# HGRN2/RWKV-7 trunk on Trainium2: where PE issues the RWKV side products around the inverse's levels, and where DVE makes the HGRN2 states

## The reference, cut to what matters

```
def step(state, inp):
    rt, wt, kt, vt, kkt, at = inp
    sa = jnp.einsum('bhvk,bhk->bhv', state, -kkt)
    state = state * wt[:, :, None, :] + sa[..., None] * (kkt * at)[:, :, None, :] + vt[..., None] * kt[:, :, None, :]
    return state, jnp.einsum('bhvk,bhk->bhv', state, rt)
```

```
o = jnp.einsum('bhts,bhsv->bhtv', attn, vc) + jnp.einsum('bhtk,bhkv->bhtv', qc * jnp.exp(G), state)
state = jnp.exp(g_last[:, :, 0, :, None]) * state + jnp.einsum('bhsk,bhsv->bhkv', kc * jnp.exp(g_last - G), vc)
```

## Time and profile before

| | us |
|---|---|
| median of 3 runs (lowest, highest) | 1282.61 (1280.92, 1283.79) |
| the profiled execution's own time | 1283.81 |
| its span, from the first to the last instruction | 1281.7 |
| PE busy in it | 1160.3 (91%) |
| DVE, POOL, ACT busy | 756.7, 618.4, 440.1 |

### The profile page before, as it was taken

The page is one execution under the profiler, slowest core; times in us unless marked ns, Lnnn a source line. Parts: engine busy times, 40 slices in busy tenths (PEclk is TensorE's granted clock), DMA queues, the critical chain, the costliest instruction groups (busy, mean ns, idle before and its releaser), DMA issues.

```text
span 1281.7 us, 31323 instructions
## 1 busy us (share of the span) xinstructions
PE 1160.3 (91%) x12058; PEld 927.3 (72%) x12058; DVE 756.7 (59%) x1344; ACT 440.1 (34%) x827; POOL 618.4 (48%) x584
## 2 busy tenths in 40 slices
PE   2898999999999999999996889997899999989995
PEld 1777877778778777787784768876677777768873
DVE  7556575475565754756554331348656776867547
ACT  4342343242422423334324410123425243442223
POOL 3643442443425424434242147777456574738771
PEclk9999999999999999999998979999899999999997
DMA  5221121211112212111121033333122222212321
GB/s 200 75 68 43 54 65 29 73 53 42 54 41 67 62 28 66 51 42 60 35 68 48 27 115 110 96 91 90 54 78 83 68 88 65 82 57 83 92 89 65
DMA packets 46726, 88.39 MB, mean 69 GB/s; under 512 B 5808, under 2 KB 6832, under 8 KB 46384
## 3 DMA queue, kind: packets, MB, share of 16 engines
q1 hardware_dynamic: 44352, 82.37, 21.9%
q10 hardware_dynamic: 2288, 4.72, 1.1%
HBM read 84.97 MB, written 2.10 MB: 68 GB/s over the span
## 4 chain that ended last, share of the span: by engine, by line
PE 73%; DVE 16%; issue 5%; ACT 4%; DMA 1%; DVEq 0%; SPq 0%; ACTq 0%
PE psum L329 72%; ACT mix L950 4%; DVE mix L1366 3%; DVE mix L1390 2%; DVE mix L1461 1%; PE psum L887 1%; DVE mix L1892 1%; DVE mix L1810 1%; DVE h_split L1370 1%; DVE mix L1821 1%; DVE mix L1884 1%; DVE mix L1875 1%; DVE mix L1890 1%; DMA mix<-xT 1%; DVE y L1896 1%
## 5 line engine op out<-in xcount | busy, mean ns | idle before, releaser
L329 PE MATMUL psum<-h_split,w_hi 128*128 128x512 f32 x2320 | 750.8, 405 | 31.2 <-DVE mix L1468 12.8
L329 PEld LDWEIGHTS psum<-h_split,w_hi 128*128 128x128 f32 x2320 | 429.2, 191 | 141.4 <-issue 42.2
L312 POOL TENSOR_SCALAR w_hi<-w_raw 128x512 fp32r<-128x512 f32 x290 | 208.1, 718 | 613.2 <-PE psum L329 472.8
L329 PE MATMUL psum<-h_split,w_lo 128*128 128x512 f32 x1160 | 457.6, 394 | 0.0
L314 POOL TENSOR_TENSOR w_lo<-w_raw,w_hi 128x512 fp32r<-128x512 f32 x290 | 410.8, 1417 | 24.2
L329 PE MATMUL psum<-mix 64*64 64x64 f32 (+5 forms) x8256 | 282.1, 238 | 40.8 <-DVE mix L1461 15.0
L329 PEld LDWEIGHTS psum<-mix 64*64 64x64 f32 (+3 forms) x8256 | 241.2, 139 | 97.3 <-issue 69.4
L950 ACT ACTIVATE mix<-psum 128x512 f32<-128x512 f32 (+4 forms) x292 | 139.9, 495 | 432.6 <-PE psum L329 323.1
L329 PEld LDWEIGHTS psum<-h_split,w_lo 128*128 128x128 f32 x1160 | 220.5, 190 | 48.5
L950 ACT ACTIVATE mix<-mix 128x512 f32<-128x512 f32 (+2 forms) x266 | 137.8, 549 | 196.9 <-DVE mix L1793 73.5
L1461 DVE COPY_PREDICATED mix<-mask,psum 128x128 f32<-128x128 uint8 (+1 forms) x192 | 83.0, 469 | 70.1 <-PE psum L329 56.2
(11 more groups left out here) (115 smaller groups left out, 658.4 us busy)
## 6 DMA issues: line engine op xcount, KB each, us to landing
w_raw<-wall SPq DMA_DIRECT2D x290, 256.0 KB, 2.6
mix<-xT SPq DMA_DIRECT2D x4, 512.0 KB, 5.4
mix<-xT ACTq DMA_DIRECT2D x1, 2048.0 KB, 8.0
out<-mix SPq DMA_DIRECT2D x8, 256.0 KB, 2.1
mix<-mask_f SPq DMA_DIRECT2D x1, 1728.0 KB, 11.1
mix<-pT ACTq DMA_DIRECT2D x2, 512.0 KB, 4.0
mix<-lru_w ACTq DMA_DIRECT2D x4, 256.0 KB, 3.4
mix<-w2a ACTq DMA_DIRECT2D x16, 32.0 KB, 2.1
```

The lines of the kernel that those rows point to most:

```text
L312: pool.tensor_scalar(w_hi[:, slot, :, :], w_raw[:, slot, :], 1.0, 0.0, ALU.mult, ALU.add).then_inc(sem["w_hi"], 1)
L329: return pe.matmul(o, lhsT, rhs, start=start, stop=stop, skip_group_check=True)
```

## The change

PE's order around the inverse, with the loop written out; `products(r, k_t)` is cut into two halves (`key_products`), two `token_rows` and `value_rows` go between levels; the `pe.sem_inc(tile_groups, 1)` of eleven functions and the semaphore are gone (shown once):

```diff
-                    for n in range(4):
-                        token_rows(r, n, head)
+                    token_rows(r, 0, head)
+                    token_rows(r, 1, head)
                     inverse_pt(r, 1, 0)
                     inverse_pt(r, 1, 1)
-                    products(r, k_t)
-                    with pe.Fori(1, 5) as lvl:
+                    key_products(r, 0)
+                    inverse_n(r, 1, 0)
+                    inverse_n(r, 1, 1)
+                    key_products(r, 1)
+                    for lvl in range(2, 5):
+                        inverse_pt(r, lvl, 0)
+                        inverse_pt(r, lvl, 1)
+                        if lvl == 4:
+                            value_rows(r)
                         inverse_n(r, lvl, 0)
                         inverse_n(r, lvl, 1)
-                        inverse_pt(r, lvl + 1, 0)
-                        inverse_pt(r, lvl + 1, 1)
-                    value_rows(r)
-                    state_sums(r, True)
+                        if lvl < 4:
+                            token_rows(r, lvl, head)
+                    inverse_pt(r, 5, 0)
+                    inverse_pt(r, 5, 1)
                     inverse_last(r, 0)
                     inverse_last(r, 1)
+                    state_sums(r, True)
                     output_sums(r, True)
```

The token rows in the order v, b, k, a, in banks 1, 0, 1, 0 (so that `inverse_pt` of level 1 needs none of them), and the new functions:

```diff
-                elif n == 3 and head:
-                    pe.wait_ge(sem["free0"], freed(r + 1, 2))
                 elif n == 1:
-                    pe.wait_ge(sem["rw_ops"], count("rw_ops", r, 3))
-                    pe.wait_ge(sem["hg_n"], count("hg_n", r))
-                o = bank[(1, 4, 5, 0)[n]]
+                    if head:
+                        pe.wait_ge(sem["free0"], freed(r + 1, 2))
+                else:
+                    pe.wait_ge(sem["rw_tok"], count("rw_tok", r, n - 2))
+                    if n == 2:
+                        pe.wait_ge(sem["rw_ops"], count("rw_ops", r, 3))
+                o = bank[(1, 0, 1, 0)[n]]
...
+            def scores(r, keys, p):
+
+                for e in range(2):
+                    for g in range(2):
+                        last = mm(bank[2 + e][rows[g], p * P:(p + 1) * P], keys[rows[e], tokens(2 * p + g)], ar[rows[e], g, p, :, :])
+                return last
...
+            def key_products(r, half):
+
+                if half == 0:
                     pe.wait_ge(sem["rw_masked"], count("rw_masked", r, 2))
-                pe.sem_inc(tile_groups, 1)
...
+                    pe.wait_ge(sem["rw_ops"], count("rw_ops", r, 3))
+                for p in (2 * half, 2 * half + 1):
+                    last = scores(r, k_t, p)
+                if half:
+                    last.then_inc(sem["rw_qk"], 1)
```

DVE has `upto` ahead of its first `inverse_pt` copy, and the states ahead of v's lerp:

```diff
+                    upto(r)
                     inverse_pt(r, 1, 0)
-                    upto(r)
                     inverse_pt(r, 1, 1)
...
+                    states(i)
                     mixed(i, 2, 7, wv)
-                    states(i)
```

More of the change, by code:

```diff
@@ L135, in trunk @@
         stored = ctx.enter_context(nc.semaphore("stored"))
-        tile_groups = ctx.enter_context(nc.semaphore("tile_groups"))
         vector_copies = ctx.enter_context(nc.semaphore("vector_copies"))
@@ L445, in token_rows @@
                         last = mm(o[:, at], wv[:, at], centre)
-                    elif n == 2:
+                    elif n == 3:
                         g, grp = p // 2, p % 2
@@ L449, in token_rows, with products @@
                     else:
-                        last = pe.transpose(o[:, at], (k_t if n == 1 else b_t)[:, at], ident)
+                        last = pe.transpose(o[:, at], (b_t if n == 1 else k_t)[:, at], ident)
                 last.then_inc(sem["rw_tr"], 1)
[L453 to L459, removed]
-                    pe.wait_ge(sem["rw_masked"], count("rw_masked", r, 2))
-                pe.sem_inc(tile_groups, 1)
[L462 to L467, removed]
+            def scores(r, keys, p):
[3 more added lines that the diff above has]
+                return last
+            def products(r):
+                pe.wait_ge(sem["rw_ops"], count("rw_ops", r, 2))
+                if not is_first(r):
+                    pe.wait_ge(sem["rw_norm"], count("rw_norm", r - 1, 0))
+                for p in range(4):
+                    last = scores(r, b_t, p)
+                last.then_inc(sem["rw_qk"], 1)
+            def key_products(r, half):
+                if half == 0:
+                    pe.wait_ge(sem["rw_masked"], count("rw_masked", r, 2))
+                    pe.wait_ge(sem["rw_ops"], count("rw_ops", r, 3))
+                for p in (2 * half, 2 * half + 1):
+                    last = scores(r, k_t, p)
+                if half:
+                    last.then_inc(sem["rw_qk"], 1)
             def turned_products(r):
@@ L490, in inverse_pt @@
             def inverse_pt(r, lvl, grp):
-                if isinstance(lvl, int) and lvl == 1:
-                    if grp == 0:
-                        pe.wait_ge(sem["rw_tok"], count("rw_tok", r, 2))
+                if lvl == 1 and grp == 0:
+                    pe.wait_ge(sem["hg_n"], count("hg_n", r))
                 pe.wait_ge(sem["rw_x"], count("rw_x", r, 2 * (lvl - 1) + grp))
-                pe.sem_inc(tile_groups, 1)
                 for e, q, g, p in in_group(grp):
@@ L526, in value_rows @@
                 pe.wait_ge(sem["rw_masked"], count("rw_masked", r, 4))
-                pe.wait_ge(sem["rw_tok"], count("rw_tok", r, 3))
-                pe.sem_inc(tile_groups, 1)
+                pe.wait_ge(sem["rw_tok"], count("rw_tok", r, 0))
                 for grp in range(2):
                     for e, q, g, p in in_group(grp):
-                        last = mm(bank[g][rows[q], P * grp + 64 * e:P * grp + 64 * e + 64], rw_m[rows[g], e, p, 4, :],
+                        last = mm(bank[2 + g][rows[q], P * grp + 64 * e:P * grp + 64 * e + 64], rw_m[rows[g], e, p, 4, :],
                                   v_tok[rows[g], e, p, :])
@@ L535, in state_sums @@
             def state_sums(r, first):
-                pe.sem_inc(tile_groups, 1)
+                if first:
+                    pe.wait_ge(sem["rw_ge"], count("rw_ge", r))
+                    pe.wait_ge(sem["rw_tok"], count("rw_tok", r, 2))
                 for p in range(4):
@@ L691, in embedding @@
                         if m == 2:
-                            pe.wait_ge(sem["rw_ge"], count("rw_ge", r))
+                            pe.wait_ge(sem["rw_tok"], count("rw_tok", r, 3))
                         embed(0, m, U_PRJ0, (0, 1))
@@ L713, in even_round @@
                 if pair:
-                    products(r, b_t)
+                    products(r)
                     turned_products(r)
-                    for n in range(4):
-                        token_rows(r, n, head)
+                    token_rows(r, 0, head)
+                    token_rows(r, 1, head)
                     inverse_pt(r, 1, 0)
                     inverse_pt(r, 1, 1)
-                    products(r, k_t)
-                    with pe.Fori(1, 5) as lvl:
+                    key_products(r, 0)
[7 more added lines that the diff above has]
+                            value_rows(r)
                         inverse_n(r, lvl, 0)
                         inverse_n(r, lvl, 1)
-                        inverse_pt(r, lvl + 1, 0)
-                        inverse_pt(r, lvl + 1, 1)
-                    value_rows(r)
-                    state_sums(r, True)
+                        if lvl < 4:
+                            token_rows(r, lvl, head)
+                    inverse_pt(r, 5, 0)
+                    inverse_pt(r, 5, 1)
                     inverse_last(r, 0)
                     inverse_last(r, 1)
+                    state_sums(r, True)
                     output_sums(r, True)
@@ L1050, in token_rows @@
                 act.wait_ge(sem["rw_tr"], count("rw_tr", r, n))
-                if n == 2:
-                    f(ga.rearrange("p g r e s t -> p (g r e) s t")[:, :, 1, :], bank[5].rearrange("p (c t) -> p c t", t=64),
+                if n == 3:
+                    f(ga.rearrange("p g r e s t -> p (g r e) s t")[:, :, 1, :], bank[0].rearrange("p (c t) -> p c t", t=64),
                       ACT.Copy).then_inc(sem["rw_tok"], 1)
                     return
-                dst = (v_tok, rw_m[:, :, :, 3, :], None, rw_m[:, :, :, 2, :])[n]
-                f(dst, bank[(1, 4, 5, 0)[n]].rearrange("p (c e t) -> p e c t", e=2, c=4), ACT.Copy).then_inc(sem["rw_tok"], 1)
+                dst = (v_tok, rw_m[:, :, :, 2, :], rw_m[:, :, :, 3, :])[n]
+                f(dst, bank[(1, 0, 1)[n]].rearrange("p (c e t) -> p e c t", e=2, c=4), ACT.Copy).then_inc(sem["rw_tok"], 1)
             def inverse_pt(r, lvl, grp):
@@ L1066, in value_rows @@
                 f(ga.rearrange("p g r e s t -> p g (r e) s t")[:, :, :, 0, :],
-                  psum[:, 0:2, 0:256].rearrange("p g (n t) -> p g n t", t=64), ACT.Copy).then_inc(sem["rw_ge"], 1)
```

(8 more changed lines are left out.)

9 lines of the change are left out of this document (1 added, 8 removed).

## The result

| | us | ratio to before, 95% interval |
|---|---|---|
| before, median of 8 runs | 1282.57 | |
| changed, median of 8 runs (1270.95 to 1278.22) | 1276.23 | 0.9943 [0.9926, 0.9961] |
| predicted | 1256.5 (1240 to 1274) | |

What follows compares the result with a forecast made beforehand. It took PE's waits for copies and masks in the inverse's serial levels, and for DVE's states at round ends, as the bound. 1283.8 - 23 (parts 1 to 3) - 11 (states) + 8 (fetch) = 1257.8, 1256.6 against the median; range 1240 to 1274.

Steps and rivals of the forecast that it cites:

- Part 5: Instruction fetching on PE: written-out inverse takes 51 packets, 14 stops of 0.87 us, 8 us more than now (-4 to +41).
- Part 2: Levels 2 to 4 of the inverse: branch's 0.2 us a level gone, moved pieces fit the waits; cost 0.1 us a round.
- Part 1: Ahead of the levels: second token rows to level 2 goes from 5.8 to 3.0 us, gain 2.8 us a round.
- rival B: Levels: fillers do not fit, token rows and `value_rows` add their whole 1.8 us a round; 1270 us; chance 0.15.
- Part 3: Behind level 5: `value_rows`' 0.48 us gone, `inverse_last` waits some 0.3 us for copies; gain 0.2 us a round.
- Part 4: End of a round: DVE makes the states before the lerp, last products start earlier; gain 1.4 us a round, 11 us.
- A: Short-product bursts: with no loop PE's stops vanish, fetch term -4 us; 1244.6 us; chance 0.22.
- C: Straight code: each of 51 packets stops PE, 44 us less today's 4; 1289 us, slower; chance 0.06.

Runs made afterwards that it cites:

- states_only: The kernel before with only DVE's states moved ahead of v's lerp: 1268.2 us, ratio 0.9893 [0.9878, 0.9907].

## Why the prediction was wrong

- **Part 5, the fetching of instructions, is the step that failed.** The mechanism was named, and the count of packets came out as forecast (18 more). The number of stops was mis-sized: 14 were taken, out of 51 packets. In the changed kernel's trace there are 22 of more than 0.4 us, 19.8 us in sum, against the five of 3.8 us before. Their length was right (0.90 us on average, 0.87 taken). So the term of +8 us measured 16 us by the prediction's own way of counting, 14 us by PE's whole "issue" time, 21 us by the stops between weight loads; and the direct comparison of a written-out and a looped levels 2 to 4 gives 21 us for 12 packets. All lie inside its range of -4 to +41. The 14 had no row under it, only the thought that stops fall in bursts. The rows could have said more: the earlier trace rows show a stop behind a packet, and 192 instructions in a level's 2.4 us ask for a packet each 3.2 us.
- **The increments.** Part 2 put them inside the 0.2 us of the branch. In straight code they are worth 19 and 20.5 us; by taking them out the change saved itself from being 14 us slower than before. So large a term stood nowhere in the sum. It acts on the stops of part 5, and without it the miss would have been 20 us larger.
- **Part 1, the part ahead of the levels**, forecast at 2.8 us a round, measured 2.2 (8.3 to 6.1) in the round read. Right in kind. The sum was 3.0 us from the second token rows to level 2 and 3.6 were measured. `upto`, ACT's copies and the wait for `hg_n` cost nothing.
- **Part 2, the levels**, forecast at 2.4 to 2.45 us with the pieces in them: 2.65 and 2.6 where PE doesn't stop. That is 0.25 and 0.2 us over the 2.40 before, for pieces of 0.67 and 0.48 us that rival B had adding their whole time: about four tenths of it, although the branch's 0.2 us had gone. A switch of tile size was put at 0.12 us; from the last weight load of token rows to the first small one it is 0.31 us (360.39 to 360.70), where the former follow each other after 0.11, so 0.2.
- **Part 3**: 372.18 to 378.61 is 6.43 us, less the stops of 1.11 and 0.52 and what they delay; the 0.2 us can't be read from it. Parts 1 to 3 were to give 23 us; the stretches without their stops lost 18. With part 5's 13 us (21 for 8), less the 2 us that part 4 gave beyond its forecast, that makes 16 of the 20 us by which the forecast missed; the rest is not accounted for.
- **Part 4, the states**: forecast 11 us, 1.4 a round; measured 12.7 and 13.5. Right in mechanism and size: a round's end lost 1.5 us, 12 us in eight. What `states_only` gained beyond it are fewer stops in the inverse, which the move of the states was not meant for.
- **The base.** One round was read for eight, and it was the shortest, by 1 us below the mean, with no stop in it. Eight times that round is 160 us, where the eight took 167; 7 us of the difference are the stops of the others, which part 5 counts, so little of the miss lies here.
- **The rivals.** A (no stops in straight code) is refuted by the 22 stops. By the Trainium skill, page "Runtime: NRT & Kernel Launch", section "Instruction fetch mechanics", a crossing into the next block is mostly hidden and a taken branch out of the fetched blocks stalls. Here taking the branches out made the kernel 35 us slower, so for dense short products the measurement decides against it. C had the right mechanism, and about half of its size came true (20 to 28 of its 44 us).
- **A correction.** The text ahead of the prediction says that rounds 2 to 7 are a loop on each engine. On PE they are written out, and the loop over the levels was the only one in its even layer; the steps of the prediction did not rest on it.

**What stays open.** That the stops are waits for instructions is shown by when they end, by the loss from written-out code at an unchanged order, and by the gain from wide matmuls between short ones. Why the increments lengthen the stops was not isolated, and the lower clock can have only a part of it. No view here shows when PE asks for its next packet.

## What to carry to other kernels

In this kernel a stretch of many short float32 products was paced by the fetch of its instructions once it was straight code: keep a loop there if one exists, or put long matmuls between the short ones, as long as they cover no wait where they stand now, and count 16 KB packets against the time before writing a loop out. Read the "issue" time of all instances of a stretch, not of one, and test a change's mechanical side effects (here a semaphore increment) by themselves: one can outweigh the reordering.

## What the runs showed of the hardware

- Written out, four passes of a loop of 192 short instructions cost 35 us in eight rounds, 4.4 us each, with no other change.
- In all fourteen traces, between 100 and 730 us, two packets of instructions never started less than 3.2 us apart. 256 instructions in 3.2 us are 13 ns each; the short products issue two in 15 ns. One packet's transfer took 1.1 us on average. The 207 stops of more than 0.4 us that no semaphore ended all ended 2.15 to 2.9 us after a packet's start. In the changed kernel's inverse at 357 to 379 us the packets follow each other every 3.6 to 3.8 us.
- A semaphore increment on PE's own queue that nobody waits for: nine functions' worth of them cost 1.8 us in all beside the loop over four passes; six a round ahead of the shorter loop cost 6.9 us; all of them in straight code 19 to 20.5 us.
- The granted clock was at its lower level (0.50, 1.2 GHz) for 13.7 to 17.1 us of the rounds in the three kernels with straight code and increments, and for at most 3.4 us in the eleven others.
